# Two-layer conditioned transformer on one core: the modulation weights of each feed-forward's gate in units of their own

## The reference, cut to what matters

```
mod = (cond @ w_mod[l] + b_mod[l])          # cond = silu(c), w_mod[l] is 1024 x 6144
sh_a, sc_a, g_a, sh_f, sc_f, g_f = split(mod, 6)
h = rms_norm(x, norm_mix[l]) * (1 + sc_a) + sh_a
x = x + g_a * (attention mixer(h) @ w_out[l])
h = rms_norm(x, norm_ffn[l]) * (1 + sc_f) + sh_f
x = x + g_f * ((silu(h @ w_gate[l]) * (h @ w_up[l])) @ w_down[l])
```

## Time and profile before

| | us |
|---|---|
| median of 3 runs | 2826.4 |
| lowest, highest | 2821.2, 2827.0 |
| span of the profiled execution | 2825.6 |
| TensorE matmul busy | 2741.9 (97%) |
| TensorE weight load busy | 2337.7 (83%) |
| VectorE busy | 2110.5 (75%) |
| ScalarE busy | 1391.3 (49%) |

### The profile page before, as it was taken

One profiled execution on the slowest core, in us unless ns is written; L12 is line 12 of the kernel. 1 busy time (PEld: TensorE's weight loads), 2 busy tenths in 40 slices (PEclk: granted clock), 3 DMA queues, 4 the chain that ended last, 5 costly groups with the idle time before them and its releaser, 6 DMA issues.

```text
span 2825.6 us, 39948 instructions
## 1 busy us (share of the span) xinstructions
PE 2741.9 (97%) x16410; PEld 2337.7 (83%) x16410; DVE 2110.5 (75%) x3118; ACT 1391.3 (49%) x1630; POOL 205.5 (7%) x172
## 2 busy tenths in 40 slices
PE   8879999999999999999999999999999999999998
PEld 7667888788888888888888888897888888888887
DVE  7777877675555579999879955546699989799655
ACT  4454445554456555554444344465555544444443
POOL 0200002010013001110000000030011100000000
PEclk9999999999999999999999999999999999999999
DMA  8847864545553355554455555633455554455554
GB/s 330 293 179 276 312 213 171 204 178 190 191 208 135 134 177 181 191 182 165 164 174 188 175 194 194 228 135 134 167 177 193 183 176 164 161 194 169 192 194 142
DMA packets 75637, 537.41 MB, mean 190 GB/s; under 512 B 8512, under 2 KB 8896, under 8 KB 12096
## 3 DMA queue, kind: packets, MB, share of 16 engines
q1 hardware_dynamic: 75456, 534.86, 54.0%
HBM read 527.48 MB, written 7.34 MB: 189 GB/s over the span
## 4 chain that ended last, share of the span: by engine, by line
PE 62%; issue 22%; DVE 7%; ACT 5%; DMA 2%; POOL 1%; SPq 0%; DVEq 0%; POOLq 0%; ACTq 0%
PE banks L447 18%; PE banks L455 9%; PE banks L521 7%; PE banks L523 7%; PE banks L531 6%; DVE wlo L1496 3%; ACT whi L1010 2%; PE banks L495 2%; PE banks L497 2%; PE banks L506 1%; PE banks L469 1%; PE banks L471 1%; PE banks L479 1%; DMA raw<-in_wkv 1%; PE banks L955 1%
## 5 line engine op out<-in xcount | busy, mean ns | idle before, releaser
L1010 ACT ACTIVATE whi<-raw 128x2048 fp32r<-128x2048 f32 x438 | 839.0, 1916 | 970.8 <-issue 803.1
L1496 DVE TENSOR_TENSOR wlo<-raw,whi 128x2048 fp32r<-128x2048 f32 x438 | 1012.1, 2311 | 309.2 <-ACT whi L1010 308.8
L447 PE MATMUL banks<-ht,whi 128*128 128x512 f32 x2880 | 702.9, 393 | 5.9 <-DVE big L1581 3.0
L447 PEld LDWEIGHTS banks<-ht,whi 128*128 128x128 f32 x2880 | 526.5, 188 | 110.0 <-issue 3.9
L521 PE MATMUL banks<-whi,ht 128*128 128x512 f32 x1152 | 457.1, 397 | 13.5 <-DVE ht L1571 9.0
L523 PE MATMUL banks<-whi,ht 128*128 128x512 f32 x1152 | 450.3, 391 | 0.0
L455 PEld LDWEIGHTS banks<-ht,wlo 128*128 128x128 f32 x2880 | 369.1, 191 | 14.5
L455 PE MATMUL banks<-ht,wlo 128*128 128x256 f32 x2880 | 373.4, 283 | 0.0
L531 PE MATMUL banks<-wlo,ht 128*128 128x512 f32 x1152 | 287.5, 389 | 0.0
L521 PEld LDWEIGHTS banks<-whi,ht 128*128 128x128 f32 x1152 | 217.1, 188 | 59.2 <-issue 14.6
L531 PEld LDWEIGHTS banks<-wlo,ht 128*128 128x128 f32 x1152 | 216.2, 188 | 45.0
(11 more groups left out here) (278 smaller groups left out, 3359.2 us busy)
## 6 DMA issues: line engine op xcount, KB each, us to landing
raw<-in_pu SPq DMA_DIRECT2D x128, 1024.0 KB, 4.9
raw<-in_pv SPq DMA_DIRECT2D x128, 1024.0 KB, 4.9
raw<-in_win SPq DMA_DIRECT2D x52, 1024.0 KB, 4.9
big<-in_wmod SPq DMA_DIRECT2D x24, 1024.0 KB, 6.4
raw<-in_wmod SPq DMA_DIRECT2D x24, 1024.0 KB, 5.1
raw<-in_wgate SPq DMA_DIRECT2D x22, 1024.0 KB, 5.0
raw<-in_wup SPq DMA_DIRECT2D x22, 1024.0 KB, 5.0
raw<-in_wdown SPq DMA_DIRECT2D x22, 1024.0 KB, 5.0
```

Of the source, the lines that this page charges most:

```text
L447: m = e.matmul(bank[b + n], h[:, q, c[n]], M.both[:, q * 512:(q + 1) * 512], start=q == 0, stop=False, skip_group_check=True)
L1010: e.activation(whi(j), slot[u][0], ACT.Copy).then_inc(*hi.mark(j))
L1496: e.tensor_tensor(wlo(j), slot[u][0], whi(j).bitcast(F32), ALU.subtract).then_inc(*lo.mark(j))
```

## The change

The two modulation rows of `c` = 2 are taken apart. `sc_f` stays `c` = 2 and `g_f` becomes `c` = 3, and each is laid out in memory so that a 1 MB unit holds two 128-row pieces of 1024 columns: four units each, 16 m units for `c` = 2 and 3 in two layers, as before. VectorE handles such a unit in two instructions of 1024 columns, the second waiting for the first.

The places of all m units change. In weight-unit positions of the lists: mixer 0 had m units behind 0, 1, 3, 4, 6, 7, 9, 10, 11 and then 12, 12, 13, 13, 14, 14, 15, and now has 12, 13, 14 in place of the latter; feed-forward 0 had 16 and has 12; mixer 1 had 8 (behind 3, 8, 11, 12, 13, 14, 15, 21) and has 12 (behind 1, 2, 4, 5, 7, 8, 10, 11, 13, 15, 17, 19); feed-forward 1 had none and has 4, in the main ring. Gate row (1, 0) moves from the start of mixer 1 into its output projection, and (0, 1) and (1, 1) move from the start of their feed-forward behind the `up` unit of its eighth step (`i == 7`).

```diff
     def munits(l, c):
-        return [("m", a["wmod"][l, c, k], l, c, k) for k in range(8)]
+        return [("m", a["wmod"][l, c, k], l, c, k) for k in range(8)] if c < 2 else [
+            ("m", a["wmod2"][l, c - 2, j], l, c, j) for j in range(4)]
...
-    units += first_mixer(0, [0, 1, 3, 4, 6, 7, 9, 10, 11, 12, 12, 13, 13, 14, 14, 15], munits(0, 1) + munits(0, 2))
-    units += ffn[0][0:1] + spread(ffn[0][1:], munits(1, 0) + munits(1, 1))
-    units += first_mixer(1, [3, 8, 11, 12, 13, 14, 15, 21], munits(1, 2)) + ffn[1]
+    units += first_mixer(0, [0, 1, 3, 4, 6, 7, 9, 10, 11, 12, 13, 14], munits(0, 1) + munits(0, 2))
+    units += ffn[0][0:1] + spread(ffn[0][1:], munits(0, 3) + munits(1, 0))
+    units += first_mixer(1, [1, 2, 4, 5, 7, 8, 10, 11, 13, 15, 17, 19], munits(1, 1) + munits(1, 2))
+    units += ffn[1][0:1] + spread(ffn[1][1:], munits(1, 3))
...
         def gate_row(l, g, bs=(None, None), part=(0, 1)):
-            on.wait_ge(*mac.at((l, 1 + g, 7)))
+            on.wait_ge(*mac.at((l, 3, 3) if g else (l, 1, 7)))
...
             else:
-                gate_row(1, 0, (0, 1))
                 warm(name, 6)
                 turn_all(name, XA, DG[0])
...
                 if i == 1:
-                    if stage == ("mix1", 0):
-                        gate_row(0, 0, (4, 5))
+                    if stage[0] == "mix1":
+                        gate_row(stage[1], 0, (4, 5))
...
         def feed_forward(l):
             name = ("ffn", l)
-            gate_row(l, 1, (0, 1))
             warm(name, 6)
             turn_all(name, XA, DG[0])
...
+                if i == 7:
+                    b = banks.where["g", l, i]
+                    gate_row(l, 1, (b, b + 1))
                 if i:
                     down(i - 1)
...
+            if c < 2:
+                part(MACC[l, c], r, k, (l, c, k))
                 return
-            on.wait_ge(*mac.at((l, c, k - 1)))
-            e.scalar_tensor_tensor(MACC[l, c], r, co, MACC[l, c], ALU.mult, ALU.add).then_inc(*mac.mark((l, c, k)))
+            part(MACC[l, c], r[:, 0:1024], 2 * k, (l, c, k, "first"))
+            on.wait_ge(*mac.at((l, c, k, "first")))
+            part(MACC[l, c], r[:, 1024:2048], 2 * k + 1, (l, c, k))
+
+        def part(to, r, k, key):
+            co = COND[:, k:k + 1]
+            if k == 0:
+                e.tensor_scalar(to, r, co, None, ALU.mult).then_inc(*mac.mark(key))
+            else:
+                e.scalar_tensor_tensor(to, r, co, to, ALU.mult, ALU.add).then_inc(*mac.mark(key))
```

More of the change, by code:

```diff
@@ L247, in program @@
     GATE = [ag(2048 + 1024 * g, 1024) for g in range(2)]
-    MACC = {(l, c): ag(4096 if (l, c) in ((0, 2), (1, 1)) else 6144, 2048) for l in range(DEPTH) for c in range(3)}
+    MACC = {(0, 0): ag(6144, 2048), (0, 1): ag(6144, 2048), (0, 2): ag(4096, 1024), (0, 3): ag(5120, 1024),
+            (1, 0): ag(6144, 2048), (1, 1): ag(4096, 2048), (1, 2): ag(6144, 1024), (1, 3): ag(7168, 1024)}
     SIDE = [ag(13312, UN), ag(15360, UN)]
@@ L279, in program @@
     lead = [u for u, x in enumerate(units) if x[0] == "m" and x[2:4] == (0, 0)]
-    side = [u for u, x in enumerate(units) if x[0] == "m" and x[2:4] in ((1, 0), (1, 1))]
+    side = [u for u, x in enumerate(units) if x[0] == "m" and x[2:4] in ((0, 3), (1, 0))]
     main = [u for u in range(len(units)) if u not in {*lead, *side}]
@@ L412, in column_turns @@
                 on.wait_ge(*mac.at((l, 1, 7)))
-                on.wait_ge(*mac.at((l, 2, 7)))
+                on.wait_ge(*mac.at((l, 2, 3)))
             else:
@@ L424, in gate_row @@
         def gate_row(l, g, bs=(None, None), part=(0, 1)):
-            on.wait_ge(*mac.at((l, 1 + g, 7)))
+            on.wait_ge(*mac.at((l, 3, 3) if g else (l, 1, 7)))
+            src = MACC[l, 3] if g else MACC[l, 1]
             for q in part:
                 b = clear(("mg", l, g, q), bs[q])
-                e.matmul(bank[b][:, :], ONES, MACC[l, 1 + g][:, g * 1024 + q * 512:g * 1024 + (q + 1) * 512], start=True,
-                         stop=True).then_inc(*modsum.mark((l, "gate", g, q)))
+                e.matmul(bank[b][:, :], ONES, src[:, q * 512:(q + 1) * 512], start=True, stop=True).then_inc(*modsum.mark((l, "gate", g, q)))
         def take():
@@ L710, in project @@
                 if i == 1:
-                    if stage == ("mix1", 0):
-                        gate_row(0, 0, (4, 5))
+                    if stage[0] == "mix1":
+                        gate_row(stage[1], 0, (4, 5))
                     for q in (2, 3):
-                        out_part(name, o, q, 4 + q if stage == ("mix1", 0) else None)
+                        out_part(name, o, q, 4 + q if stage[0] == "mix1" else None)
         def feed_forward(l):
             name = ("ffn", l)
-            gate_row(l, 1, (0, 1))
             warm(name, 6)
@@ L1498, in through @@
                     modulate(u, *units[u][2:])
-        reused = {(0, 1): (0, 0), (1, 0): (0, 1, 3), (1, 1): (0, "gate", 1, 1), (1, 2): (1, 0, 3)}
+        reused = {(0, 1): (0, 0), (1, 0): (0, 1, 3), (1, 1): (0, "gate", 1, 1), (1, 2): (1, 0, 3), (1, 3): (1, 0, 3)}
         def modulate(u, l, c, k):
-            r, co = slot[u][0], COND[:, k:k + 1]
+            r = slot[u][0]
             landed(on, u)
@@ L1508, in modulate @@
                     on.wait_ge(*modsum.at(reused[l, c]))
-                e.tensor_scalar(MACC[l, c], r, co, None, ALU.mult).then_inc(*mac.mark((l, c, k)))
+            else:
+                on.wait_ge(*mac.at((l, c, k - 1)))
+            if c < 2:
+                part(MACC[l, c], r, k, (l, c, k))
                 return
-            on.wait_ge(*mac.at((l, c, k - 1)))
-            e.scalar_tensor_tensor(MACC[l, c], r, co, MACC[l, c], ALU.mult, ALU.add).then_inc(*mac.mark((l, c, k)))
+            part(MACC[l, c], r[:, 0:1024], 2 * k, (l, c, k, "first"))
[5 more added lines that the diff above has]
+                e.tensor_scalar(to, r, co, None, ALU.mult).then_inc(*mac.mark(key))
+            else:
+                e.scalar_tensor_tensor(to, r, co, to, ALU.mult, ALU.add).then_inc(*mac.mark(key))
         def columns(l, part):
@@ L1700, in first_mixer @@
                 take()
[L1701 to L1706, removed]
+                if l == 0 and nb == 0:
+                    rotations()
+                    lambdas()
                 if l and nb == 3:
@@ L1802, in first_mixer @@
             out_parts(("o1", l), l, (2, 3))
-            if l == 0:
-                gate_row(0, 0)
+            gate_row(l, 0)
             take()
@@ L1826, in feed_forward @@
                 upto(k + 2)
-                if i == 0:
-                    gate_row(l, 1)
                 joined(gate, ("g", l, i))
@@ L1838, in feed_forward @@
                     columns_summed(1, 0, (2 * i - 16, 2 * i - 15))
+                if i == 7:
+                    gate_row(l, 1)
                 if (l, i) == (0, 9):
@@ L2647, in lay_out @@
         "bgate": asc(bias[:, [2, 5]]),
-        "wmod": asc(v["w_mod"].reshape(L, 8, P, 3, UN).transpose(0, 3, 1, 2, 4)),
+        "wmod": asc(v["w_mod"].reshape(L, 8, P, 3, UN)[:, :, :, 0:2].transpose(0, 3, 1, 2, 4)),
+        "wmod2": asc(v["w_mod"].reshape(L, 4, 2, P, 6, 1024)[:, :, :, :, 4:6].transpose(0, 4, 1, 3, 2, 5)).reshape(
+            L, 2, 4, P, UN),
         "win": b_form(w), "wout": c_form(v["w_out"]), "wgate": a_form(v["w_gate"]), "wup": a_form(v["w_up"]),
```

## The result

| | before | after |
|---|---|---|
| median, us | 2825.3 (19 runs) | 2830.3 (19 runs) |
| lowest, highest | 2820.3, 2827.8 | 2826.0, 2833.9 |
| span of the profiled execution | 2825.6 | 2826.6 |

The ratio is 1.0019 with an interval of 1.0012 to 1.0025: 5.4 us slower (3.4 to 7.1), a loss that is clear of zero and about as large as the 0.2% of the prediction's chances. The forecast was 2829, which was 2.5 above the 2826.4 that before's first three runs gave; the change came out about twice as large as forecast.

What follows compares the result with a forecast made beforehand. TensorE, busy 97% of the span, was taken as the bound, so only its gaps could pay. The terms, -7.5 + 5.1 + 1.1 + 0.4 + 3.4 = +2.5 us on 2826.4, gave about 2829, range 2820 to 2836.

Steps and rivals of the forecast that it cites:

- the 0.2% of the prediction's chances: Whole kernel: within 0.2% (5.7 us) counts as hardly different; chances faster 0.10, within 0.63, slower 0.27.
- A: Attention of mixer 0: seven m units become three packed ones, sparing waits and clock episodes; -7.5 us.
- B: Three gate rows leave gaps at stage starts for full stages, each costing 1.71 us of TensorE; +5.1 us.
- C: Attention of mixer 1: a new m unit before a low part outlasts its 1.50 us of idle time; +1.1 us.
- D: Projection of mixer 1: 8 m units where 3 were make one load 0.2 to 0.5 us late; +0.4 us.
- E: Starts of mixer 1 and both feed-forwards: longer gaps lower the clock in both feed-forwards, not mixer 1; +3.4 us.
- The four takes: Attention of mixer 0: four places where fewer m units shorten the path, by 1.7, 1.0, 1.7 and 0.7 us.
- the 2.4 us of the clock: Attention of mixer 0: two half-clock episodes go as the first and third gap shrink, at 1.2 us each.
- The fast rival: Attention of mixer 0 is bound by VectorE alone, all four gaps shrink, clock holds at starts; 2817.4 us, chance 0.10.
- the sign of being wrong: Projection of mixer 1: TensorE waits for the high part's copy (line 495 for line 1010) would appear.
- that rival: The ring starves mixer 1's projection as in mixer 0, costing 6.9 us; 2835.4 us, chance 0.15.
- The rival in which the clock holds: The longer gaps at the three starts cost no clock; sum -0.9, 2825.5 us, chance 0.18.

Runs made afterwards that it cites:

- the eight above: Eight follow-up kernels, each a variation of the kernel before or of the changed one; measured at 2820.6 to 2831.5 us.
- light list: Changed kernel with eight m units of mixer 1 back beside feed-forward 0 and gate row (0,1) at its fourth step: 2826.0 us, ratio 1.0002.
- longer warming: Changed kernel with ten instead of six warm-up matmuls at the starts of mixer 1 and both feed-forwards: 2827.7 us, ratio 1.0006.
- shorter warming: Changed kernel with two instead of six warm-up matmuls at the starts of mixer 1 and both feed-forwards: 2828.5 us, ratio 1.0017.

## Why the prediction was right, and which terms were off

The stages are measured from the first row of one to the first of the next on TensorE, in ten traces: the kernel before, the changed one and the eight above. Those with the same list for a stage are averaged.

| term | forecast | measured | from |
|---|---|---|---|
| A, attention of mixer 0 | -7.5 | -5.9 | 66.7 (2 traces, 67.4 and 66.1) to 60.9 (8 traces, 59.7 to 63.9) |
| B, gate rows | +5.1 | +5.0 | 1.74 and 1.51 in the feed-forwards, 1.71 in the output projection |
| C, attention of mixer 1 | +1.1 | +1.4 | with the unit behind 17: 76.7 (5 traces); without: 75.3 (5) |
| D, projection of mixer 1 | +0.4 | +1.2 | dense list: 78.1 (5 traces, 76.6 to 79.6); old or light: 76.9 (5, 76.5 to 78.2) |
| E, clock at three starts | +3.4 | +3.1 | worked out below |
| sum | +2.5 | +4.8 | the runs: +5.4 (3.4 to 7.1) |

The mechanism named in each term is there. Two terms are off in size: A, by the part that the clock was to give back, and D; C, B and E are within 0.3.

That the time itself was met so closely (2829 forecast, 2830.3 measured) is in part luck. The forecast started from 2826.4, the median of three runs; over 19 it is 2825.3. As a change, +2.5 was forecast and +5.4 measured, and +2.5 lies outside the interval of 3.4 to 7.1.

**A.** The four takes came out as they were summed; the step that failed is the 2.4 us of the clock. The stage can be cut at waits that every trace has, and each piece timed from the end of one wait to the end of the next (us; the first piece from the stage's first row). The fourth column compares traces with the same clock in that piece, first with before's list of m units, then with the changed kernel's:

| up to the end of | before | after | same clock, old and new list | forecast |
|---|---|---|---|---|
| the first wait for a softmax (take 1) | 12.86 | 11.19 | 12.9, 11.2 | -1.7 |
| a wait of 0.9 us for a copy, at 166 us in before (take 2) | 19.66 | 18.34 | 19.6, 18.4 | -1.0 |
| the second wait for a softmax (take 3) | 5.49 | 3.82 | 5.5, 3.8 | -1.7 |
| a wait of 0.7 us for a copy, at 183 us in before | 11.96 | 10.37 | 10.4, 10.4 | 0 |
| the long wait for a copy, 3.1 us in before (take 4) | 5.84 | 5.17 | 5.8, 5.2 | -0.7 |
| the wait for VectorE's combination | 6.30 | 6.29 | 6.3, 6.3 | 0 |
| the output projection | 5.32 | 5.72 | | 0 |

At the same clock the takes bring 1.7 + 1.2 + 1.7 + 0.7 = 5.2 us, the 5.1 of the forecast. The clock brought 1.2 in this pair: 1.6 in the fourth piece, which had a stretch at half clock in before and in none of the eight traces with the new list, less 0.4 in the last piece. Over all traces it brought 5.9 - 5.2 = 0.7. The forecast took two of four episodes to go, at 1.2 each. But behind the first wait, shrunk to 0.9 us and with one of 0.8 us just behind it, the clock still fell in four of the eight traces. And an episode costs nothing as far as it lies in the piece that ends with VectorE's combination: that piece takes 6.29 to 6.31 us in all ten traces, with anything from 0.1 to 3.15 us of full-clock work lost in it; the wait inside it is 4.0 us where the matmuls in front ran at full clock and 2.2 to 3.6 where some of them did not. The fast rival, VectorE as the only bound (2817.4), asked for over 12.2 us in this stage, which gave 5.9, and is refuted.

**B.** Each row costs its 1.7 us on TensorE, and with the rows moved alone the loss is there. Three rows that lay in gaps, for nothing, now lie in full stages. Nothing else in the change is as certain or as large on the side of loss.

**C.** The idle time in front of the low part was the cover, 1.50 us, and a unit of 2.60 us overran it by 1.1. The longer wait, 4.1 for 3.2 us, is 0.9 of it, and among the traces with one short stretch of low clock in the stage it is the whole difference: 76.0 to 76.1 us with the unit (three traces), 75.1 to 75.2 without (four). The rest of the 1.4 is the clock's, which fell for longer in two of the five with the unit and in one of the five without. In the pair before and after it doesn't show at all (76.06 and 76.07 us), since the longer gap was offset by a shorter stretch at the lower clock.

**D.** One late load was forecast, 0.2 to 0.5 us late. It is there, and later: in four of the five traces with the dense list TensorE has one wait of 0.8 to 1.0 us for a high part, and in the fifth, and in all five with the old or the light list, none. That is the sign of being wrong that the prediction named, in one wait and not in several as in mixer 0. At full clock the stage takes 77.7 us with such a wait (two traces) and 76.5 to 76.6 without (five), so it costs 1.1. A third trace has a longer wait in front of the attention too, 2.6 for 1.5 us, and takes 78.9. The pair before and after alone would put D at +3.0 (76.56 to 79.58), near the 3.6 from which that rival decides; most of the rest of it is a stretch at half clock, and the one trace with the old list that has such a stretch takes 78.2. The light list's kernel was 4.8 us faster by the ratios than the changed one, with an uncertainty of 3.1; C does not differ between the two, and their traces show 1.2 on average for D and 0.3 to 0.6 in feed-forward 0. Whether the rest is more than scatter is not settled.

**E.** Two episodes as forecast, at places that were not. Over all traces of this study: behind a gap of 2.7 us at a start the clock fell in 8 of 9 cases (not at feed-forward 0 of the changed kernel's profile), behind 2.2 us in 3 of 5, behind 1.0 or less in none of 13. An episode costs 1.2 to 1.5 us at these starts, not 1.7. So E = 0.89 x 1.35 x 2 + 0.6 x 1.2 = 3.1. The ten warming matmuls brought back 3.7 us by the ratios (with an uncertainty of 3), the same within it, and all three starts to their old lengths. The rival in which the clock holds is refuted. The Trainium skill (TensorE: Matmul & The Clock Gate, The HAM clock gate) says that the gate's windows run free of the kernel's start. The traces fit that, and don't prove it: 2.18 us lost the clock in one program and 2.20 did not in another, and 2.71 us went both ways at the same start.

**Why the two profiles hid the loss.** Ten traces have the same program up to the attention of mixer 0. Its projection takes 79.3 us in the profile of before, the longest of the ten, and 74.4 in that of after, nearly the shortest (74.3). That is 4.9 us in after's favour, nearly all of it in waits: TensorE waited 6.5 us for high parts there in before and 2.6 in after, and ScalarE 23.6 and 16.3 us for the loads. The attention of mixer 0 gave 6.5 in this pair, 0.6 more than the averages say. The second block, untouched, took 1.4 us more. Together they make 1.0 of the spans out of a loss of 5 in the medians.

**Where the scatter comes from.** The second block is the same in all ten traces and takes 2019.1 to 2023.8 us in them. The order is that of its stretches at half clock (the one at the very end, which all have, not counted): with one 2019.1, with two 2020.6 and 2020.7, with three 2022.0 to 2022.2 (four traces), with four 2023.5 to 2023.8 (three traces). They lie at five places of the program, and each goes with about 1.5 us. TensorE by 2 us at the first of these places that longer warming has at half clock, and at the same place with shorter warming, the trace that has only one:

```profile
1012.00:1014.00 2.00, 1.69 (x5) 0.53 1.02 317
...
1008.00:1010.00 2.00, 1.16 (x4) 1.00 1.03 358
```

So 4.7 us of difference in a block that nobody changed go with the clock, which fell at a place in one execution and not in another.

**Open.** Why the projection of mixer 0 varies by 5 us in the same program, at full clock in both of the pair. Loads in it land after a median of 4.9 to 6.8 us; the two longest stages, 79.3 and 77.1, go with 6.8 and 5.0, so the landing doesn't order them. The modulation weights lie elsewhere in memory in the changed kernel, which no run takes apart from the rest. And why the same gap costs the clock in one execution and not in the next.

## What to carry to other kernels

A matmul that stands in a gap of TensorE is free, and the gap is also shorter for the clock by it; before moving one out, count what it costs in the full stage and what the longer gap does to the clock. If it must move, put more dummy matmuls in its place. A wait that grew need not be a loss: time the piece from the end of one wait to the end of the next. Price a clock episode by where it lies: in front of VectorE's combination here it cost nothing, at the starts 1.2 to 1.5 us. Changes of a few us are to be read from averages over several traces of a stage: one pair put 4.9 us of chance into an unchanged one.

## What the runs showed of the hardware

The same program's weight loads of 1 MB in the projection of mixer 0 took a median of 5.4 us from issue to landing in the profile of after (4.8 to 7.4):

```profile
DMA to landing us min/median/max: 4.8/5.4/7.4
```

In before's it was 6.8, on the same list of loads. Even the shortest of the earlier trace rows, 4.7, lies above the 4.4 us that were estimated by the Trainium skill (DMA: Bandwidth & Descriptors, Anatomy of one DMA); that section is on DMAs issued by gpsimd, and these loads are issued by SyncE. A gap of 1.7 us followed by transposes was followed by a half-clock stretch in the projection of mixer 1 in two of the ten traces (at 470 us in after, at 467 us with four m units of mixer 0 left out), where the same gap left the clock alone in the other eight. And a stretch at half clock in front of a wait for VectorE cost nothing, with 6.30 us for that piece of the stage in every trace.
